# Gating expert rows as they leave PSUM and adding them by indirect DMA into a DRAM table, in a mixture-of-experts encoder step

## What is computed

```python
h = yp + jnp.concatenate([gm, sb], axis=-1) @ w_out[l]
yp = h + hier_moe(rmsnorm(h, norm2_g[l]), *moe_args)
# in hier_moe: top-1 of 4 groups, top-2 of the 4 experts in it
gates = p_sel[:, None] * top_v / jnp.sum(top_v, axis=-1, keepdims=True)
hg = jnp.einsum('nd,edf->nef', xf, w_gate)
hu = jnp.einsum('nd,edf->nef', xf, w_up)
a = jax.nn.silu(hg) * hu * combine[:, :, None]
y = jnp.einsum('nef,efd->nd', a, w_down)
```

## Time and profile before

| | us |
|---|---|
| median of 3 runs (528.54 to 532.43) | 529.55 |
| span of the profiled execution | 529.8 |

### The profile page before, as it was taken

One profiled execution on the slowest core, in us unless ns is written; L12 is line 12 of the kernel. 1 busy time (PEld: TensorE's weight loads), 2 busy tenths in 40 slices (PEclk: granted clock), 3 DMA queues, 4 the chain that ended last, 5 costly groups with the idle time before them and its releaser, 6 DMA issues. The chain is left out here.

```text
span 529.8 us, 7155 instructions
## 1 busy us (share of the span) xinstructions
PE 448.5 (85%) x2569; PEld 333.4 (63%) x2569; DVE 291.5 (55%) x411; ACT 241.3 (46%) x330; POOL 194.1 (37%) x189
## 2 busy tenths in 40 slices
PE   1899999998979899999999961689999999999300
PEld 1677887777758576656777861466766766666200
DVE  2626332443243446565150747269898898998136
ACT  4625121343333536456113531167787777876100
POOL 3442100474540000001000761266767767746261
PEclk9999999998979999999999986599999999999855
DMA  8547202222331300000297397359999999993267
GB/s 300 165 72 280 62 24 81 83 77 80 119 125 56 109 1 1 1 1 1 90 390 275 128 354 242 91 191 338 342 348 330 331 344 316 362 366 131 85 228 277
DMA packets 61700, 95.31 MB, mean 180 GB/s; under 512 B 9265, under 2 KB 42033, under 8 KB 61665
## 3 DMA queue, kind: packets, MB, share of 16 engines
q1 hardware_dynamic: 47040, 69.48, 38.7%
q0 software_dynamic: 5088, 17.89, 10.4%
q10 hardware_dynamic: 9536, 7.50, 4.3%
HBM read 81.82 MB, written 13.04 MB: 179 GB/s over the span
## 5 line engine op out<-in xcount | busy, mean ns | idle before, releaser
L1272 DVE TENSOR_TENSOR wlo<-raw,whi 128x2048 fp32r<-128x2048 f32 (+1 forms) x45 | 96.9, 2154 | 24.4 <-ACT whi L866 24.4
L1384 PE MATMUL bank<-whi,xT_hi 128*128 128x512 f32 x224 | 93.6, 418 | 2.5 <-issue 1.9
L1385 PE MATMUL bank<-wlo,xT_hi 128*128 128x512 f32 x224 | 90.8, 405 | 0.0
L1386 PE MATMUL bank<-whi,xT_lo 128*128 128x512 f32 x224 | 90.8, 405 | 0.0
L866 ACT ACTIVATE whi<-raw 128x2048 fp32r<-128x2048 f32 x45 | 86.0, 1912 | 6.2 <-PE bank L1386 6.2
L591 POOL TENSOR_TENSOR wlo<-raw,whi 128x1024 fp32r<-128x1024 f32 x16 | 59.6, 3724 | 34.4 <-ACT whi L866 34.4
L953 DVE TENSOR_TENSOR wlo<-raw,whi 128x2048 fp32r<-128x2048 f32 x14 | 32.0, 2287 | 52.6 <-ACT whi L657 52.6
L1384 PE MATMUL bank<-whi,xsT_hi 128*96 128x512 f32 x128 | 53.4, 417 | 4.4 <-DVE xsT_lo L1278 3.1
L1384 PEld LDWEIGHTS bank<-whi,xT_hi 128*128 128x128 f32 x224 | 43.6, 195 | 14.6 <-issue 4.2
L1386 PE MATMUL bank<-whi,xsT_lo 128*96 128x512 f32 x128 | 51.4, 402 | 0.0
L1385 PE MATMUL bank<-wlo,xsT_hi 128*96 128x512 f32 x128 | 51.3, 401 | 0.0
(11 more groups left out here) (214 smaller groups left out, 773.2 us busy)
## 6 DMA issues: line engine op xcount, KB each, us to landing
raw<-in_w_gate_dram SPq DMA_DIRECT2D x32, 512.0 KB, 6.3
raw<-in_w_up_dram SPq DMA_DIRECT2D x32, 512.0 KB, 7.8
raw<-in_w_down_dram SPq DMA_DIRECT2D x32, 512.0 KB, 7.2
raw<-in_w_in_dram SPq DMA_DIRECT2D x10, 1024.0 KB, 5.4
expert_rows<-yout POOLq DMA_DIRECT2D x16, 384.0 KB
raw<-in_w_out_dram SPq DMA_DIRECT2D x4, 1024.0 KB, 5.1
x_sb<-in_x_prompt_dram SPq DMA_DIRECT2D x4, 512.0 KB, 8.8
normed_tokens<-xn ACTq DMA_DIRECT2D x4, 512.0 KB, 2.7
```

The source lines that it names most:

```text
L1272: dve.tensor_tensor(wlo[SPLIT_OF[m3]][:, 0:n], eraw[slot][:, 0:n], whi[SPLIT_OF[m3]][:, 0:n].bitcast(F32), ALU.subtract).then_inc(m_lo, 1)
L1384: pe.matmul(acc, x_hi, w_hi, start=start, stop=False)
L1385: pe.matmul(acc, x_hi, w_lo, start=False, stop=False)
L1386: return pe.matmul(acc, x_lo, w_hi, start=False, stop=stop)
```

## The change

The table `expert_rows` is replaced by `summed_rows`, which holds the residual rows: 544 token rows and 96 spare rows.

- SP stores `x_sb` into it (six transfers, 2.6 MB) between the units 7 and 8 of the weights.
- DVE computes two more slot tables: `to_all` (for each slot the row to add to; an empty slot gets a spare row) and `slot_gate` (the gate of the slot's token). The gates go through a second one-hot product on PE, cut in three bf16 pieces whose sum is the gate. The computation of `pos_y` is gone.
- ACT and DVE multiply by `slot_gate` as they copy `yout` out of PSUM.
- POOL's plain store of `yout` becomes a copy of one column of `to_all` and an indirect DMA that adds the 96 rows to `summed_rows`. Each add waits until the add before it has landed, since the same token may stand in both.
- The fetch by POOL, the sums on DVE and the stores from `x_sb` are gone. When the last adds have landed, SP copies `summed_rows` to the two outputs, from DRAM to DRAM.

```diff
@@ SP, moe_loads
                 for m in range(NRAW):
                     first(m)
+                    if isinstance(r, int) and m == 7:
+                        for t in range(NT):
+                            sp_.wait_ge(acc_free[t], 3)
+                            sp_.dma_start(sum_dram[tok(t), :], x_sb[0:rows[t], t, :]).then_inc(h_st, 16)
+                        sp_.dma_start(sum_dram[TOK:TOK + CAP, :], x_sb[0:CAP, 0, :]).then_inc(h_st, 16)
...
-            for t in range(NT):
-                sp_.wait_ge(y_ok, t + 1)
-                dst = y_prompt[0, tok(t), :] if t < NT - 1 else y_sample[0, :, :]
-                sp_.dma_start(dst, x_sb[0:rows[t], t, :]).then_inc(y_out, 16)
-            sp_.wait_ge(y_out, 16 * NT)
+            sp_.wait_ge(all_added, 1)
+            sp_.dma_start(y_prompt[0, :, :], sum_dram[0:SEQ, :]).then_inc(y_out, 16)
+            sp_.dma_start(y_sample[0, :, :], sum_dram[SEQ:TOK, :]).then_inc(y_out, 16)
+            sp_.wait_ge(y_out, 32)
@@ POOL, moe_gathers
-                def store(i, p):
+                def add_rows(i, p, n):
                     s = s0 + i
+                    if isinstance(i, int) and i == 0:
+                        pool.wait_ge(to_ok, r + 1)
+                        pool.sem_inc(pool_tick, 1)
+                    pool.tensor_copy(to_cur[p], to_all[:, bass.ds(i, 1)]).then_inc(to_cp, 1)
+                    pool.wait_ge(to_cp, s + 1)
                     pool.wait_ge(y_act, s + 1)
                     pool.wait_ge(y_dve, s + 1)
-                    pool.dma_start(y_dram[bass.ds(r * SLOTS + i * CAP, CAP), :], yout[p][:, :]).then_inc(y_st[p], 16)
+                    if isinstance(s, int) and s == 0:
+                        pool.wait_ge(h_st, 16 * (NT + 1))
+                    else:
+                        pool.wait_ge(y_st[1 - p], 16 * ((E // 2) * r + n))
+                    pool.sem_inc(pool_tick, 1)
+                    pool.indirect_dma_start(sum_dram[:, :], bass.IndirectOffsetOnAxis(ap=to_cur[p], axis=0),
+                                            yout[p][:, :], None, compute_op=ALU.add).then_inc(y_st[p], 16)
...
-                fetch(ROUNDS * SLOTS)
-            with pool.Else():
-                fetch(SLOTS)
+            pool.sem_inc(all_added, 1)
@@ ACT, out_rows
-                    act.activation(yout[p][:, 0:CB], bank[2][0:CAP, :], ACT.Copy).then_inc(y_act, 1)
+                    act.activation(yout[p][:, 0:CB], bank[2][0:CAP, :], ACT.Copy, scale=slot_gate[:, bass.ds(i, 1)])\
+                       .then_inc(y_act, 1)
@@ DVE
+                dve.tensor_tensor(ids_of[:, c * NT:(c + 1) * NT, 2 * E:3 * E], s2[c], wide(valid, E), ALU.mult)
...
+                dve.tensor_scalar(idx_free, bank[4][0:CAP, 2 * E:3 * E], spare_row[0:CAP, 1:2], spare_row[0:CAP, 0:1],
+                                  ALU.mult, ALU.add).then_inc(to_half, 1)
+                dve.wait_ge(to_half, 2 * r + 1)
+                dve.tensor_tensor(idx_free, idx_free, idx_rows, ALU.add).then_inc(to_half, 1)
+                dve.wait_ge(to_half, 2 * r + 2)
+                dve.tensor_tensor(to_all, idx_free, bank[4][0:CAP, E:2 * E], ALU.add).then_inc(to_ok, 1)
...
+            dve.wait_ge(h_st, 16 * (NT + 1))
+            link(dve.tensor_tensor(gate_left[:, :, :], sel_all, gate_b, ALU.mult))
+            for a in range(3):
+                piece = gates_of[:, :, a * E:(a + 1) * E]
+                ins = dve.tensor_copy(piece, gate_left[:, :, :])
+                if a < 2:
+                    link(ins)
+                    link(dve.tensor_tensor(gate_left[:, :, :], gate_left[:, :, :], piece, ALU.subtract))
+            ins.then_inc(gates_ok, 1)
...
-                    dve.tensor_copy(yout[p][:, CB:D], bank[3][0:CAP, :]).then_inc(y_dve, 1)
+                    dve.tensor_scalar(yout[p][:, CB:D], bank[3][0:CAP, :], slot_gate[:, bass.ds(i, 1)], None, ALU.mult).then_inc(y_dve, 1)
...
-            for t in range(NT):
-                p = rows[t]
-                dve.wait_ge(yg_ld[t], 32)
-                for c in range(2):
-                    ins = dve.scalar_tensor_tensor(out=x_sb[0:p, t, :], in0=yg[c][t][0:p, :], scalar=gate[c][0:p, t:t + 1],
-                                                   in1=x_sb[0:p, t, :], op0=ALU.mult, op1=ALU.add)
@@ PE
+            def gate_table(r):
+
+                pe.wait_ge(gates_ok, 1)
+                pe.wait_ge(to_ok, r + 1)
+                for m in range(2 * NT):
+                    mm = pe.matmul(bank[4][0:CAP, 3 * E:6 * E], onehot[:, m, :], gates_of[:, m, :], start=(m == 0), stop=(m == 2 * NT - 1))
+                mm.then_inc(gates_mm, 1)
...
+                gate_table(r)
                 turn_tokens(0, 0, 0)
```

More of the change, by code:

```diff
@@ L112, in trunk_step @@
         selb = sb("selb", [P, NT, E], BF16)
-        gate = [sb(f"gate{i}", [P, NT]) for i in range(2)]
+        gate = sb("gate", [P, 2, NT])
         rank_of = [sb(f"rank_of{i}", [P, NT]) for i in range(2)]
-        pos_y = [sb(f"pos_y{i}", [P, NT], I32) for i in range(2)]
+        spare_row = sb("spare_row", [P, 2])
         cnt = sb("cnt", [P, 1])
         flag = sb("flag", [P, 1], I32)
-        idx_all = sb("idx_all", [CAP, E], I32)
-        idx_cur = [sb(f"idx_cur{i}", [CAP, 1], I32) for i in range(2)]
         mix = ExitStack()
@@ L158, in trunk_step @@
         r16 = sb("r16", [P, NT, NG, EPG], stack=st_c)
-        sel = [sb(f"sel{i}", [P, NT, NG, EPG], stack=st_c) for i in range(2)]
+        sel = sb("sel", [P, 2, NT, NG, EPG], stack=st_c)
         st_c.close()
@@ L179, in trunk_step @@
         aT_lo = [sb(f"aT_lo{i}", [P, 2, CAP], F32R) for i in range(2)]
-        ids_of = sb("ids_of", [P, 2 * NT, 2 * E], BF16)
+        ids_of = sb("ids_of", [P, 2 * NT, 3 * E], BF16)
         onehot = sb("onehot", [P, 2 * NT, CAP], BF16)
-        idx_rows = sb("idx_rows", [CAP, E])
-        yg = [[eraw[t][:, c * D:(c + 1) * D] for t in range(NT)] for c in range(2)]
+        idx_rows, idx_free, slot_gate = (kg[0:CAP, c * E:(c + 1) * E] for c in range(3))
+        idx_all, to_all = (qg[0:CAP, c * E:(c + 1) * E].bitcast(I32) for c in range(2))
+        idx_cur = [qg[0:CAP, 2 * E + i:2 * E + i + 1].bitcast(I32) for i in range(2)]
+        to_cur = [qg[0:CAP, 2 * E + 2 + i:2 * E + 3 + i].bitcast(I32) for i in range(2)]
         xn2_of = [xn2[t % 2][:, :] for t in range(NT - 1)] + [xn2_late[:, :]]
@@ L513, in _ @@
             for a in range(2):
-                pool.affine_select(out=tok_part[:, a, :], in_=tok_part[:, a, :], compare_op=ALU.is_ge, fill=0.0, base=TOK - 1,
-                                   pattern=[[-P, NT]], channel_multiplier=-1)
+                link(pool.affine_select(out=tok_part[:, a, :], in_=tok_part[:, a, :], compare_op=ALU.is_ge, fill=0.0, base=TOK - 1,
+                                        pattern=[[-P, NT]], channel_multiplier=-1))
+            for c, sign in enumerate((1.0, -1.0)):
+                pool.tensor_scalar(spare_row[:, c:c + 1], tok_part[:, 0, 0:1], sign, sign * TOK, ALU.mult, ALU.add)
             link(pool.memset(valid[:, :], 1.0))
@@ L577, in gather @@
                         pool.sem_inc(pool_tick, 1)
[L578 removed]
+                    pool.tensor_copy(idx_cur[p], idx_all[:, bass.ds(i, 1)]).then_inc(idx_cp, 1)
                     pool.wait_ge(idx_cp, s + 1)
@@ L606, in step @@
                     if not (isinstance(i, int) and i < 2):
-                        store(i - 2, p)
+                        add_rows(i - 2, p, half_of(i - 1, j, 2 + a))
                 gather(0, 0)
@@ L1263, in _ @@
-            ins.then_inc(places_ok, 1)
+            link(dve.reciprocal(gate[:, 0, :], r1[8][:, :]))
+            link(dve.tensor_tensor(gate[:, 0, :], gate[:, 0, :], valid[:, :], ALU.mult))
+            link(dve.tensor_tensor(gate[:, 1, :], gate[:, 0, :], r1[5][:, :], ALU.mult))
+            sel_all = sel[:, :, :, :, :].rearrange("p c t g e -> p (c t) (g e)")
+            gate_b = gate[:, :, :].rearrange("p c (t a) -> p (c t) a", a=1).broadcast_to([P, 2 * NT, E])
+            dve.wait_ge(h_st, 16 * (NT + 1))
@@ L1628, in slot_table @@
                 for m in range(2 * NT):
-                    mm = pe.matmul(bank[4][0:CAP, 0:2 * E], onehot[:, m, :], ids_of[:, m, :], start=(m == 0), stop=(m == 2 * NT - 1))
+                    mm = pe.matmul(bank[4][0:CAP, 0:3 * E], onehot[:, m, :], ids_of[:, m, :], start=(m == 0), stop=(m == 2 * NT - 1))
                 mm.then_inc(ids_mm, 1)
+            def gate_table(r):
[4 more added lines that the diff above has]
+                mm.then_inc(gates_mm, 1)
             def moe(r):
```

75 lines of the change are left out of this document (34 added, 41 removed).

## The result

| | before | changed | ratio |
| --- | --- | --- | --- |
| median of the runs | 529.35 us | 540.71 us (539.62 to 541.23) | 1.018 [1.014, 1.022] |
| start to the tokens' transposes for the first expert | 334.74 | 331.60 | |
| expert loop, from there to the last matmul's end | 161.48 | 182.62 | |
| end stage | 33.58 | 23.58 | |
| span of the profiled execution | 529.8 | 537.8 | |

What follows compares the result with a forecast made beforehand. It took a ring of POOL and DVE taking turns at SBUF, 9.6 us an expert, as the bound. Sum: 529.8 + 0.5 + 10.3 + 0.85 - 12.1 = 529.3 us; range for 8 in 10, 518 to 555.

Steps and rivals of the forecast that it cites:

- the ring: Expert loop: closed chain of DVE's half split, POOL's half split and DVE's full split, 9.6 us, growing to 10.55.
- the 0.94: POOL in the loop: ring 0.94 us longer an expert, gather held by DVE's half split; +10.3 us over 11 turns.
- the first rival: Loop: the gather's issue does not wait for DVE, so +2.4 us instead of +10.3, 521 us; 20%.
- The adds' wait for each other: Loop: each add waits for the previous one's landing, taken as 9 us, hidden in the 10.55 us ring.
- the second rival: Loop: adds landing later than 10.5 us stall POOL and then PE; at 12 us, 551 us in all; 25%.
- DMA, 0: Loop: the adds' extra 0.39 MB of reads an expert cost 0, since loads made ahead pay the difference.
- the third rival: Loop: weights become the bound if an add costs two further DMA passes instead of one, 537 us; 8%.
- ACT and DVE copies: Loop: copies out of PSUM keep their shapes and gain a factor, cost 0; DVE's row 0.68 us.
- Router, +0.5: Start: two more products ahead of the slot table and a wider PE product; the rest hides behind the first gather.
- Last half split, +0.85: Loop's end: column copy and add ahead of POOL's last half split make the last matmul end 0.85 us later.
- End stage, -12.1: After the last matmul: last adds 5 us each, then the DRAM-to-DRAM copy; 21.5 us instead of 33.6.
- The base: Starting point of the sum: profiled span 529.8 us, taken as agreeing with the runs' median of 529.55.

Runs made afterwards that it cites:

- e1: The changed kernel with the add's column copied early, next to the gather's, ahead of POOL's half split: 533.64 us, ratio 1.005.
- e4: The changed kernel with a plain store to a fixed place instead of the indirect add, column still copied late: 529.76 us, ratio 0.997.
- e2: The changed kernel with the add's and the gather's columns both copied ahead of POOL's half split, four buffers for the gather's column: 529.59 us, ratio 0.995.
- e7: The changed kernel with both columns copied early and plain rows written over the table's rows instead of added: 519.57 us, ratio 0.975.
- e10: The changed kernel with the add's column copied early and a plain store to a fixed place instead of the add: 517.36 us, ratio 0.973.
- e5: The changed kernel with POOL's half splits given to DVE, columns copied late as before: 523.52 us, ratio 0.983.
- e12: The kernel before the change with POOL's half splits given to DVE, nothing else changed: 525.84 us, ratio 0.990.
- e3: The changed kernel with the indirect DMA writing plain rows over the table's rows instead of adding them: 535.64 us, ratio 1.009.

## Why the prediction was wrong

The likeliest case was 529.3 us and no change; measured were 540.7 and 1.8% more. That the range (518 to 555) holds 540.7 is luck: its upper end stood for adds that land after 12.3 us, and they landed after 6.6 in the median. The parts of the sum that differ, each taken up below, account for the rest: loop +7.4 (17.7 for 10.3) and 0.7 around it, last half split +1.9, end stage +2.1, router -0.5, 11.6 us in all.

**The step that failed** is the free place in the ring. I set the add "from 0.95 to 1.9" behind DVE's full split, had the next split begin at 1.19, and priced the add at 0.94 as if it passed. It stands 0.89 to 0.97 behind the split's end, and the next split starts 1.18 behind it: 0.22 to 0.29 us of room, and five of the adds do not pass. The rows of before show a gather that passes with 0.33 (405.25, 405.58), and none with less. In the two turns of 10.65, where it passed and PE kept its clock, the ring is the one of the working, step by step: add at +0.89, column copy held by the next split, gather held by the half split (1.77), half split 2.39, a turn of 10.65 against the 10.55 worked out. A price for the other side of so small a margin (the issue held until the split ends, and 0.95 more a turn: 11 x 0.95 = 10 us) was not in the sum, nor among the rivals. With six of 11 turns at 11.6, one of them by an add that waited for a landing, the term is 17.7 us instead of 10.3. What decides between 0.22 and 0.29 us, the wait behind the copy being 0.85 or 0.92, the runs don't show.

**And the 0.94 does not need the add.** The working had the copy, its wait and 0.94 of issue push the gather's column behind DVE's next split. The store in the add's place (10.63, an issue of 0.56) shows that the late copy and its wait alone do that; the copy as such had been costed only as taking the place of another.

**The gather and DVE.** Held, as the earlier trace rows had it, so the first rival falls: 1.77 and 1.79 in the two turns of 10.65, the only ones in which it starts inside a split, and 1.66 to 1.78 in all 11 turns of e1 and e4. The Trainium skill (SBUF — State Buffer, Who interferes with whom) says that a DVE instruction with two SBUF inputs contends with a GpSimd instruction that reads SBUF; the column copy agrees with that (2.27 beside the full split, 0.17 to 0.20 alone). Of writing descriptors it infers the opposite, and here the traces disagree wherever an indirect issue meets a split: 3.82 against 1.45 for an add, 3.33 against 0.95 for plain rows, 1.76 against 0.94 for a gather. A plain store, which reads no index column, was not seen held (0.52 to 0.56 in all runs that have it); whether it is the reading of the column that is held, as the prediction argued, no run separates.

**The adds' wait for each other** was right but for one turn: landing 6.6 in the median, taken as 9. The one landing of 11.6, behind an issue that was itself held, made the next add wait, as the second rival has it; it is behind one long turn of six, some 1 us, and the rival falls as what decides. **DMA, 0:** right for this kernel, since its own longer turn gives the weights time, and ACT waits for none. As a statement on the add it was wrong: counted in bytes the turn needs as much per us as before, counted in engine time an add takes 17 engine-us more than plain rows, and at a turn of 9.9 there are 12 us of waits (e2) that plain rows do not have (e7). That is what the third rival foresaw, behind what decided.

**ACT and DVE copies:** DVE's takes 0.74 instead of 0.68, and the turn of e10 is as much longer than 9.61. **Router, +0.5:** 0 (from DVE's first sum into `x_sb` to the slot table 38.38 us, before 38.35); the cover held with 0.90 of the 1.1 us. **Last half split, +0.85:** from the last full split's end (496.55) to the last matmul's (514.22) it is 17.7 us, against 15.0 (481.24 to 496.22): 2.7, part of it because PE's last product takes 0.63 instead of 0.40; the granted clock of 508.0 to 514.3 is 0.77.

**End stage, -12.1:** -10.0. Adds 13, 14 and 15 are 6.6 and 6.7 us apart, not 5 (the fastest landing of all is 5.2): the last is issued 5.1 us behind the last matmul instead of 3.6. From there to the copies it is 8.95, worked out as 9.4, and from the copies to the end 9.6 instead of 8.5.

**The base.** The span of 529.8 and the median of 529.55 agree by chance: every run's time lies 1.6 to 2.1 us above its span (539.62 for 537.8), so the profiled execution of before took some 531.5 us. The sum loses little by it, since only differences are added to it.

## What to carry to other kernels

When the sum lets an instruction pass between two others with a margin of a few tenths, price both sides of it times the number of turns, and see that the margin is there before building on it: here a copy moved ahead of the half split was worth 7 us, and taking POOL's splits away 17 (5 in the kernel before). An indirect DMA is more than its transfer: index column, wait and issue are three steps on POOL, of which copy and issue can each be held for a whole split of DVE; that costs time when the work DVE or PE waits for stands behind them, and nothing when there is slack (e10). And a stage that is shortened at the end by traffic put into a loop whose DMA engines are full can be paid for in that loop, here once the lock is out of the way (e5 against e12).

## What the hardware showed beside that

An indirect add's issue takes 1.43 to 1.46 us on POOL when nothing holds it, that of plain rows or a gather of the same 96 rows 0.93 to 0.98 in the loop.

How much lead on DVE's split such an issue needs depends on what DVE did before. Where the split follows another instruction of DVE without a gap, all 32 issues of these runs with a lead of 0.02 to 0.26 us were held (five adds of the changed kernel, five issues of e3, 11 gathers each of e7 and e10), and none with 0.28 or 0.29 (15) or, in the kernel before, 0.33 to 0.35 (11). Where DVE had stood idle ahead of the split, by 0.19 us or more, all 12 issues with 0.01 to 0.23 passed, and the split was not longer either, as here in the changed kernel:

```profile
340.55 0.93 POOL L589 DMA_INDIRECT xs<-normed_tokens,qg  x1 [0.80 <-POOL qg L586]
```

```profile
340.78 2.29 DVE L1302 TENSOR_TENSOR wlo<-raw,whi 128x2048 fp32r<-128x2048 f32 x1 [6.04 <-ACT whi L874]
```

Why is open.

Adding to DRAM instead of writing there took the DMA engines 1.07 us of all 16 more for 384 KB. A copy of 2.2 MB from DRAM to DRAM in two transfers took 8.5 and 7.9 us from issue to landing.
